# A two-block model on one core: Fourier mixing between two small norms, weight pieces rounded ahead of the first norm, and two 512-column norms taken in two halves

## The chip, the core and the metric

The kernel runs on one core of a Trainium2 chip. TensorE (PE) multiplies, VectorE (DVE) and ScalarE (ACT) do everything between the products, GpSimd (POOL) and SyncE (SP) issue the transfers. The metric is the device time of one execution in microseconds (us); less is better.

## The reference

A first block (two kinds of attention, a cross attention, sixteen experts) makes x; a second block of two layers mixes x (256 tokens, "latent") with a context of 256 tokens. Width 1024, fp32. What the change touches lies in the second block and in the very first norm:

```python
def rmsnorm(x, g):
    y = x * lax.rsqrt(jnp.mean(x * x, axis=-1, keepdims=True) + EPS)
    return y * g

def fourier_mix(u):                       # 256 of the projection's columns
    ug = u.reshape(B, N, F_GROUPS, F_GROUP_DIM)
    return jnp.fft.fft2(ug, axes=(1, 3), norm="ortho").real.reshape(B, N, F_WIDTH)

for l in range(2):
    h  = modulate(rmsnorm(x,  g_norm1[l]), sh1,  sc1)
    hc = modulate(rmsnorm(xc, g_norm1[l]), sh1c, sc1c)
    pf, mq, mk, mv, mo, mg, cq, ckv, kr = split_proj(h @ w_in[l])      # hc likewise
    y_f = fourier_mix(pf)
    ...                                   # mLSTM of q, k, v and the gates mg, both directions
    q  = rmsnorm(cq, g_qn) @ w_uq         # attention through small norms
    kv = rmsnorm(ckv, g_kvn) @ w_ukv
    x  = x + ga1 * (concat([y_f, y_m, y_a]) @ w_out[l])
    x  = x + ga2 * (square(relu(modulate(rmsnorm(x, g_norm2[l]), sh2, sc2) @ w_up[l])) @ w_down[l])
    # layer 0 does the same for the context xc; layer 1 updates the latent half alone
```

## The kernel before

**Layout.** Features lie on the partitions, tokens along the free axis. `res`, `uh` and `ul` hold eight tiles of 128 features by 512 tokens: the slice `CTX` is the context's 256 tokens, `LAT` the latent 256, `ALL` both. Layer 0 works on ALL, layer 1 on LAT but for its keys, values and gates.

**Products in three parts.** Every fp32 weight piece (128 by 1024) is split: ACT copies it, rounded, to `wh` (`hi_part`), DVE subtracts to get the low part `wl` (`lo_part`). Activations are split into `uh` and `ul` in the same way, and `prod` issues three matmuls: high by high, high by low, low by high. The pieces come in one stream through a ring of four slots. A piece n may be rounded when PE has begun piece n-3, and be loaded when the low part of piece n-4 is written. `split(to)`, called by hand in ACT's and DVE's program, sets where in their order each piece is handled (`AHEAD` = 3 pieces before its use).

**Norms.** ACT squares the eight tiles, DVE adds the squares into one slot of `sq`, PE sums over the partitions with a product by ones into bank 7 (`norm` on PE), ACT takes Ln and Exp for `rstd` (`root`). Then DVE scales a tile (`uv`), ACT rounds it to `uh` (`round_u`), DVE makes `ul` (`rest`), and the next matmuls wait for each `ul`. `turn_over` issues matmuls on a constant tile `spin` whose results nobody reads; the table `SPIN` says how many stand before and after the sum of a norm (`"n2_0": (7, 17, 5)`: seven, seventeen, into bank 5).

**Stages that the change touches.** At the start the norm `mix` is followed by `linears("qk", ...)`; ACT's order is `root("mix")`, `split(2)` (three pieces), `round_tiles`. In each layer, after the projections, 32 small products turn the gates' rows (`gcol`), then come the norms `cq` and `ckv`, the products `uq`, `rot`, `kn`, `va`, then the Fourier mixing (`fa`, then `fy`, for each half of the tokens), then the attention's `scores`. At the end of layer 0's mixing stand the eight products `out_0`, whose results DVE adds to `res`, the norm `n2_0` over 512 columns, and `together`, which begins three pieces of the up projection tile by tile as `ul` comes. At the end of layer 0 the last eight down products (`dnb_0`, four turns of a loop in which DVE also reduces the modulation weights, `late_two`, and adds to `res`) are followed by `mod_bias(1)`, the norm `n1_1` over 512 columns, and layer 1's `together`: the gates' piece over ALL, two query pieces over LAT.

**Banks.** Products take banks 0 to 3 in the order of the list `JOBS`; a bank is claimed again once the product four places earlier was emptied.

Of the kernel before, what the change touches and what calls it, by code (L numbers as in the profile page):

```python
# [22 lines left out]
P = 128  # L23
# [71 lines left out]
for _i, (_name, _steps, _halves) in enumerate(NORM_LIST):  # L95
    NORM[_name], STEPS[_name], HALVES[_name] = _i, _steps, _halves
    SQ_AT[_name], ADD_AT[_name] = _sq, _add
    _sq += _steps
    _add += _steps if _name in LOOPED else max(_steps - 2, 0)
# [3 lines left out]
for _l in range(NL):  # L103
    if _l == 0:
        U_STEPS += [("c1_0", 8)]
    U_STEPS += [(f"n1_{_l}", 8), (f"y_{_l}", 10), (f"n2_{_l}", 8)]
# [11 lines left out]
for _name, _n in U_STEPS:  # L118
# [5 lines left out]
        "n2_0": (7, 17, 5), "n1_1": (18, 17, 6), "n2_1": (5, 8, 5),  # L124
        "cq_0": (0, 4, 6), "ckv_0": (4, 6, 6)}
TAIL_SPIN = (6, 8)


OUT_NORMS = [_name for _name, _, _ in NORM_LIST if _name not in V_N and _name not in ("fin1", "ctx")]
# [87 lines left out]
for _l in range(NL):  # L217
    _w = 2 if _l == 0 else 1
    for _phase, _count, _engine in [("mqk", 8, "act"), ("mv", 4, "act"), ("mo", 4, "act"), ("cq", 2, "act"),
                                    ("ckv", 1, "act"), ("pf", 2, "act"), ("uq", 4, "act"), ("rot", 5, "dve"),  # L220
                                    ("kn", 4, "act"), ("va", 4, "act"),
                                    ("fa0", 2, "act"), ("fy0", 2, "act"), ("fa1", 2 * (_w - 1), "act"), ("fy1", 2 * (_w - 1), "act"),
                                    ("mlstm", 4, f"mlstm{_l}"),
                                    ("out", 8, "dve"), ("upa", MC, "act"), ("dna", 8, "dve"), ("upb", MC, "act"), ("dnb", 8, "dve")]:
        JOBS.add(f"{_phase}_{_l}", _count, _engine, _phase != "mlstm")


def build(nc, w_stream, mod_stream, c_rows, ml_dram, gate_dram, table_in, small_in, x_in, mem_in, ctx_in, out):
    with ExitStack() as stack:
# [347 lines left out]
        def _(act):  # L577
# [48 lines left out]

            def round_u(name, i, parts, ready=None):
# [50 lines left out]
            act.wait_ge(S("early_in"), 16)  # L678
            root("mix", P, T, D)
            split(2)  # L680
# [181 lines left out]
            for l in range(NL):  # L862
# [3 lines left out]
                if l:  # L866
                    root(f"n1_{l}", P, 2 * T, D)
                round_mod(l, 0)
# [52 lines left out]
                for d in range(2):  # L921
# [4 lines left out]
                                   ACT.Copy).then_inc(S("gcol_in"), 1)  # L926
                root(f"cq_{l}", P, n, 256)
                square(f"ckv_{l}", 0, ckv[:, :], P, 512)
                root(f"ckv_{l}", P, 512, 128)
# [9 lines left out]
                for s in range(n // T):  # L939
                    sc = slice(cols.start + s * T, cols.start + (s + 1) * T)  # L940
                    for ft in range(2):
                        b = full(act, f"fa{s}_{l}", ft)
                        emptied(act.activation(fa[:, ft, :, :], b[:, :].rearrange("p (a t) -> p a t", a=2),
                                               ACT.Copy), "act")
                    for ft in range(2):
                        b = full(act, f"fy{s}_{l}", ft)
                        emptied(act.activation(yf[:, ft, sc], b[:, 0:T], ACT.Copy), "act")
# [69 lines left out]
                lag = l  # L1017
                for m in range(KT + lag):
                    if m < KT:
                        split(p0 + N_IN2 + min(m, KT - 2) + AHEAD)  # L1020
                    if m >= lag:
                        wait_emptied(act, f"out_{l}", m - lag)
                        square(f"n2_{l}", m - lag, res[:, m - lag, cols], P, n)
                split(p0 + N_IN2 + KT - 1 + AHEAD)
                root(f"n2_{l}", P, n, D)
                round_mod(l, 1)

                for half, name in enumerate("ab"):
# [24 lines left out]
                    else:  # L1053
                        nxt = "n1_1" if l == 0 else "fin2"

                        turns = 4 if l < NL - 1 else 3
# [16 lines left out]
                        if turns == 3:  # L1073
                            hi_at[0] = pd + 12 + AHEAD
                            split(pd + 15)
                            down_squares(3, 3)
                    hi_at[0] = pd + MC + AHEAD
# [4 lines left out]
        def _(pe):  # L1082
# [50 lines left out]
            def norm(name, p, n):  # L1133
# [19 lines left out]
                turn_over(after, spare)  # L1153

# [292 lines left out]
            for l in range(NL):  # L1447
# [3 lines left out]
                if l:  # L1451
                    norm(f"n1_{l}", P, 2 * T)

# [39 lines left out]
                else:  # L1493
                    b = [claim(f"mqk_{l}", j) for j in range(2)]
                    together(f"n1_{l}", p0 - 1, [(bank[4][:, :], P, ALL, True, "ml_g_full"),
                                                 (b[0][0:MD, 0:n], MD, cols, True, "job_full"),
                                                 (b[1][0:MD, 0:n], MD, cols, True, "job_full")])
# [23 lines left out]
                for d in range(2):  # L1521
# [5 lines left out]
                    last.then_inc(S("gcol_full"), 1)  # L1527
                norm(f"cq_{l}", P, n)
                norm_ckv = f"ckv_{l}"

                pe.wait_ge(S("norm_rstd"), NORM[f"cq_{l}"] + 1)
                norm(norm_ckv, P, 512)
# [24 lines left out]

                cn = tab("cn").rearrange("p (b n) -> p b n", b=2)
                sn = tab("sn").rearrange("p (b n) -> p b n", b=2)
                for s in range(n // T):  # L1560
                    c0 = cols.start + s * T
                    for ft in range(2):
                        b = claim(f"fa{s}_{l}", ft)
                        wait_emptied(pe, f"pf_{l}", ft)
                        for nb in range(TB):
                            last = mm(b[:, nb * T:(nb + 1) * T], pf[:, ft, c0 + nb * P:c0 + (nb + 1) * P],
                                      tab("cdsd"), start=True, stop=True)
                        finish(last)
                    for ft in range(2):
                        b = claim(f"fy{s}_{l}", ft)  # L1570
                        wait_emptied(pe, f"fa{s}_{l}", ft)
                        for nb in range(TB):
                            mm(b[:, 0:T], fa[:, ft, nb, 0:P], cn[:, nb, :], start=(nb == 0), stop=False)
                            last = mm(b[:, 0:T], fa[:, ft, nb, P:2 * P], sn[:, nb, :], start=False, stop=(nb == 1))
                        finish(last)
# [83 lines left out]
                for m in range(2, KT):  # L1659
# [5 lines left out]
                norm(f"n2_{l}", P, n)  # L1665
                for half, name in enumerate("ab"):
# [4 lines left out]
                    if half == 0:  # L1671
                        together(f"n2_{l}", pu, [(claim(f"upa_{l}", j)[:, 0:n], P, cols, True, "job_full")
                                                 for j in range(3)])
                        b = claim(f"upa_{l}", 3)
# [21 lines left out]
                    with pe.Fori(0, 4) as i:  # L1696
                        for m in range(2):
# [10 lines left out]
                            last.then_inc(S("job_full"), 1)  # L1708
            norm("fin2", P, T)
# [3 lines left out]
        def _(dve):  # L1713
# [443 lines left out]
    
            for l in range(NL):
# [3 lines left out]
                norm_mod(l, 0)  # L2162
# [198 lines left out]
                for m in range(KT):  # L2361
                    split(p0 + N_IN2 + min(m, KT - 2) + AHEAD)
                    b = full(dve, f"out_{l}", m)
                    emptied(gated(l, m, b, 2), "dve")
                    if m >= 2 + l:
                        add_square(f"n2_{l}", m - 1 - l, P, n)
                for m in range(KT - 1 - l, KT):
                    add_square(f"n2_{l}", m, P, n)
                split(p0 + N_IN2 + KT - 1 + AHEAD)
# [276 lines left out]
```

## Time and profile before

| | us |
|---|---|
| median of 3 runs | 1637.81 (1633.72 to 1641.09) |
| the profiled execution | 1635.65 |
| its span from first to last instruction | 1633.8 |
| PE busy | 1563.7 (96%) |
| DVE busy | 1059.7 (65%) |
| ACT busy | 762.2 (47%) |

PE's busy time counts matmuls of `spin` too, and it is a union of records whose ends are modelled, so 96% doesn't say that 96% of the time does useful work. Starts of neighbouring records tell more than their lengths. An fp32 product (not the split kind) shows as two records. The view of stretches gives the granted TensorE clock as a share: 1.00 is 2.4 GHz, 0.50 is 1.2 GHz.

### The profile page before, as it was taken

What the parts mean: (1) busy time and instruction counts of PE and PEld (TensorE: products, weight loads), DVE (VectorE), ACT (ScalarE), POOL (GpSimd) and SP (SyncE); (2) the same over time, 40 slices, a digit from 0 to 9 for tenths busy, and PEclk for the clock granted to TensorE, in tenths of its full rate; (3) what the DMA queues carried; (4) which work ended last, traced back from release to release, by engine and by line L of the source; (5) the groups of instructions that cost most, each with busy time, mean ns of one, the idle gap of its engine ahead of it and who ended that gap; (6) DMA issues with size and microseconds to landing.
All of it is one profiled execution on the core that took longest, in us unless ns stands there. A gap on an engine that the chain in (4) does not pass through costs nothing.

```text
span 1633.8 us, 27313 instructions
## 1 busy us (share of the span) xinstructions
PE 1563.7 (96%) x9969; PEld 1373.7 (84%) x9969; DVE 1059.7 (65%) x1794; ACT 762.2 (47%) x1309; POOL 99.5 (6%) x165
## 2 busy tenths in 40 slices
PE   7999989999999999999899999999999998999997
PEld 6998788899999997876677888888887885899997
DVE  5567487788888888724765655455557955765564
ACT  5544544444444455344653541244224455665562
POOL 0011000000000000000300100001000001100000
PEclk9999999999999999999999999999999999999999
DMA  7665154487777733330322654455442452146562
GB/s 265 216 225 183 58 178 158 130 289 245 242 245 244 256 105 116 104 90 14 65 104 64 207 191 143 141 193 185 162 154 73 139 130 39 58 159 191 176 191 90
DMA packets 71497, 253.86 MB, mean 155 GB/s; under 512 B 7888, under 2 KB 11120, under 8 KB 71168
## 3 DMA queue, kind: packets, MB, share of 16 engines
q1 hardware_dynamic: 54048, 189.43, 34.9%
q0 software_dynamic: 17376, 63.44, 13.3%
q8 instruction: 49, 0.80, 0.2%
q14 instruction: 24, 0.20, 0.0%
HBM read 251.73 MB, written 1.11 MB: 155 GB/s over the span
## 4 chain that ended last, share of the span: by engine, by line
PE 83%; DVE 10%; ACT 3%; issue 3%; DMA 1%; DVEq 0%; SPq 0%; ACTq 0%
PE pair L1087 82%; ACT wh L586 1%; DVE sq L2299 1%; DVE uv L1761 1%; DVE wl L1720 1%; DVE sq L1801 1%; DVE small L1793 1%; DVE spent L1853 1%; PE pair L1131 1%; DVE uh_f L1853 1%; PE pair L1266 1%; ACT sq L654 0%; DMA uh_f<-in_mods 0%; DMA table<-in_table 0%; DVE ul L1750 0%
## 5 line engine op out<-in xcount | busy, mean ns | idle before, releaser
L1087 PE MATMUL pair<-uh,wh 128*128 128x256 f32 (+3 forms) x1864 | 581.9, 312 | 16.5 <-DVE ul L1750 9.7
L1720 DVE TENSOR_TENSOR wl<-ring,wh 128x1024 fp32r<-128x1024 f32 x350 | 426.6, 1223 | 253.1 <-ACT wh L586 247.1
L1087 PE MATMUL pair<-ul,wh 128*128 128x256 f32 (+3 forms) x1864 | 576.2, 309 | 0.0
L1087 PE MATMUL pair<-uh,wl 128*128 128x256 f32 (+3 forms) x1864 | 576.0, 309 | 0.0
L586 ACT ACTIVATE wh<-ring 128x1024 fp32r<-128x1024 f32 x350 | 366.9, 1052 | 260.4 <-PE pair L1087 253.1
L1087 PEld LDWEIGHTS pair<-uh,wh 128*128 128x128 f32 (+1 forms) x1864 | 346.8, 186 | 45.4 <-issue 17.9
L1087 PEld LDWEIGHTS pair<-uh,wl 128*128 128x128 f32 (+1 forms) x1864 | 347.0, 186 | 23.7
L1087 PEld LDWEIGHTS pair<-ul,wh 128*128 128x128 f32 (+1 forms) x1864 | 346.9, 186 | 22.6
L1087 PE MATMUL pair<-hh,wh 128*128 128x512 f32 (+1 forms) x512 | 172.6, 337 | 0.8
L1087 PE MATMUL pair<-hl,wh 128*128 128x512 f32 (+1 forms) x512 | 172.0, 336 | 0.0
L1087 PE MATMUL pair<-hh,wl 128*128 128x512 f32 (+1 forms) x512 | 172.0, 336 | 0.0
L1087 PEld LDWEIGHTS pair<-hh,wh 128*128 128x128 f32 x512 | 97.1, 190 | 12.0 <-issue 2.0
L1087 PEld LDWEIGHTS pair<-hl,wh 128*128 128x128 f32 x512 | 97.2, 190 | 10.0
L1087 PEld LDWEIGHTS pair<-hh,wl 128*128 128x128 f32 x512 | 97.2, 190 | 9.9
L2420 DVE TENSOR_TENSOR hl<-sq,hh 128x512 f32 (+1 forms) x64 | 35.7, 558 | 92.4 <-ACT hh L1046 92.3
L1041 ACT ACTIVATE sq<-pair 128x512 f32<-128x512 f32 (+1 forms) x64 | 31.3, 489 | 104.4 <-PE pair L1087 104.3
L1087 PE MATMUL pair<-hidh,wl 128*128 128x256 f32 x256 | 72.6, 284 | 0.0
L1087 PE MATMUL pair<-hidh,wh 128*128 128x256 f32 x256 | 72.5, 283 | 0.0
L1087 PE MATMUL pair<-hidl,wh 128*128 128x256 f32 x256 | 72.4, 283 | 0.0
L1087 PE MATMUL pair<-wh,uh 128*128 128x256 f32 (+1 forms) x192 | 57.4, 299 | 3.0 <-ACT qkp L885 3.0
L516 POOL DMA_DIRECT2D uh_f<-in_mods x48 | 36.0, 750 | 397.2 <-DVE macc L1838 218.7
L1838 DVE CUSTOM_DVE_ANT_0 mod_w<-mod_w,mod_c 128x1024 f32<-128x1024 f32 x48 | 58.5, 1218 | 0.0
(279 smaller groups left out, 1991.8 us busy)
## 6 DMA issues: line engine op xcount, KB each, us to landing
ring<-in_w_stream SPq DMA_DIRECT2D x350, 512.0 KB, 3.7
uh_f<-in_mods POOLq DMA_DIRECT2D x48, 512.0 KB, 6.1
mod_w<-in_mods POOLq DMA_DIRECT2D x48, 512.0 KB, 3.8
uv<-c_rows POOLq DMA_DIRECT2D x4, 512.0 KB, 7.1
ml<-ml_dram POOLq DMA_DIRECT2D x4, 512.0 KB, 8.3
table<-in_table SPq DMA_DIRECT2D x1, 1849.5 KB, 12.2
res<-in_x SPq DMA_DIRECT2D x4, 256.0 KB, 4.1
res<-in_mem SPq DMA_DIRECT2D x1, 1024.0 KB, 14.4
```

Source lines behind the costliest of these rows:

```text
L516: pool.dma_start(dst, src).then_inc(S(f"mod_in{g % 2}"), 16)
L586: act.activation(wh[:, s, :], ring[:, s, :], ACT.Copy).then_inc(S("w_hi"), 1)
L1041: act.activation(r, bank[(b0 + j) % 4][:, 0:n], ACT.Relu).then_inc(S("job_emptied_act"), 1)
L1087: ins = pe.matmul(*operands, **flags)
L1131: pe.matmul(bank[b], spin[:, 0:P], spin[:, :], start=True, stop=True)
L1266: last = pe.transpose(bank[6][:, to * P:(to + 1) * P], prob[i % 2][:, j * P:(j + 1) * P], ident)
L1720: tt(wl[:, s, :], ring[:, s, :], wh[:, s, :].bitcast(F32), ALU.subtract).then_inc(S("w_lo"), 1)
L1761: last = stt(o, src, g, r, ALU.mult, ALU.mult)
L1793: dve.tensor_reduce(smv(i, 0, 0, g), b, AX_X, ALU.max, negate=True).then_inc(S("sm_max"), 1)
L1838: return dve.tensor_tensor_reduce(out=mod_w[l][k], in0=mod_w[l][k], in1=mod_c[l][which], scale=1.0, scalar=0.0, op0=ALU.mult, op1=ALU.add, ...
L1853: last = dve.tensor_tensor_reduce(out=w if which == 0 else spent_to, in0=w, in1=c[which], scale=1.0, scalar=0.0, op0=ALU.mult, op1=ALU.add ...
L2420: tt(hl[:, d, 0:n].rearrange("p a b -> p (a b)"), sq[:, 2 + j % 2, 0:n], hh[:, d, 0:n].rearrange("p a b -> p (a b)").bitcast(F32), ALU.sub ...
```

## The change

Four edits, and what follows from them:

- **Start.** ACT's `split(2)` stands ahead of `root("mix")`.
- **Small norms.** `JOBS` gets `fa` and `fy` ahead of `uq`, and all three engines follow. Layer 0: after the sum of `cq`, PE does `fa`, `fy` of the context; after the sum of `ckv`, `fa`, `fy` of the latent half. Layer 1: `fa` after the sum of `cq`, `fy` after the sum of `ckv`. ACT empties them between its roots. The spins of both norms in layer 0 go.
- **`n2_0` in halves.** `out_0` 6 and 7 are computed over CTX first, then over LAT into banks 4 and 5. The context's sum, root, tiles and rounding come ahead of the latent's; DVE and ACT have the last adds, squares and one `split` between them. The first three pieces of the up projection run over CTX (two of them tile by tile, then the third), then over LAT. 24 spins go.
- **`n1_1` in halves.** The loop over down products has three turns; the last turn is written out. Its second product runs over CTX, then LAT into bank 6. DVE does the last `late_two` and `mod_bias(1)` ahead of the last adds. Layer 1's gates run over CTX tile by tile, with the latent's sum after the fourth tile, then 8 spins, then gates over LAT with the two query pieces. 35 spins go, 8 come.

```diff
+            split(2)
             root("mix", P, T, D)
-            split(2)
             round_tiles("mix", LAT)
...
+            def half_sum(name, c, squares):
+                pe.wait_ge(S("norm_add"), ADD_AT[name] + (5 if name == "n2_0" else 6))
+                pe.wait_ge(S("norm_sq"), SQ_AT[name] + squares)
+                for k, slot in enumerate((3, 0, 1)):
+                    last = mm(bank[7][:, c], ones, sq[:, slot, c], start=(c is CTX and k == 0), stop=(k == 2),
+                              skip_group_check=True)
+                last.then_inc(S("half_ms" if c is CTX else "norm_ms"), 1)
...
                 norm(f"cq_{l}", P, n)
+                spectrum(0, "fa")
+                if l == 0:
+                    spectrum(0, "fy")
                 pe.wait_ge(S("norm_rstd"), NORM[f"cq_{l}"] + 1)
-                norm(norm_ckv, P, 512)
+                norm(f"ckv_{l}", P, 512)
+                if l == 0:
+                    spectrum(1, "fa")
+                    spectrum(1, "fy")
+                else:
+                    spectrum(0, "fy")
...
+                    b = {m: claim("out_0", m) for m in (6, 7)}
+                    for c in (CTX, LAT):
+                        for m in (6, 7):
...
+                            last.then_inc(S("out_ctx" if c is CTX else "job_full"), 1)
+                            if c is LAT and m == 6:
+                                half_sum("n2_0", CTX, 8)
...
+                        for k in range(KT):
+                            for j in range(2):
+                                up(j, k, CTX)
+                            if k == 2:
+                                half_sum("n2_0", LAT, 10)
+                        pe.wait_ge(S("w_lo"), pu + 3)
+                        for k in range(KT):
+                            up(2, k, CTX)
+                        for k in range(KT):
+                            for j in range(3):
...
+                                last = up(j, k, LAT)
...
+                    for k in range(KT):
+                        pe.wait_ge(S("u_l"), U_AT["n1_1c"] + k + 1)
+                        prod(bank[4][:, CTX], p0 - 1, k, uh[:, k, CTX], ul[:, k, CTX], k == 0, k == KT - 1,
+                             skip_group_check=True)
+                        if k == 3:
+                            half_sum("n1_1", LAT, 9)
+                    turn_over(8, 5)
...
+            def half_tiles(l, k2, add_last, then):          # DVE
+                half_tile(l, k2, CTX, 0)
+                half_tile(l, k2, CTX, 1)
+                half_rest(l, k2, CTX, 0)
+                half_tile(l, k2, CTX, 2)
+                half_rest(l, k2, CTX, 1)
+                add_last()
+                half_tile(l, k2, CTX, 3)
+                half_rest(l, k2, CTX, 2)
+                then()
+                for k in range(4, KT):
+                    half_tile(l, k2, CTX, k)
+                    half_rest(l, k2, CTX, k - 1)
+                for k in range(KT):
+                    half_tile(l, k2, LAT, k)
...
+                            root_half("n1_1", CTX)          # ACT
+                            round_half(1, 0, CTX, 0)
+                            round_half(1, 0, CTX, 1)
+                            split(pd + 18)
+                            act.wait_ge(S("job_emptied_dve"), b1 + 7)
+                            act.activation(sq[:, 1, LAT], res[:, 7, LAT], ACT.Square).then_inc(S("norm_sq"), 1)
+                            for k in range(2, 4):
+                                round_half(1, 0, CTX, k)
+                            root_half("n1_1", LAT)
+                            for k in range(4, KT):
+                                round_half(1, 0, CTX, k)
+                            for k in range(KT):
+                                round_half(1, 0, LAT, k)
```

`n2_0` has the same order on ACT, with `split(po + KT + 2)` in the place of `split(pd + 18)`, where `po` is the first of the `out_0` pieces.

## Rows read from the trace of the kernel before

**Rows 1.** The page: the chain that ended last, shares of the span by engine.
```profile
PE 83%; DVE 10%; ACT 3%; issue 3%; DMA 1%; DVEq 0%; SPq 0%; ACTq 0%
```
**Rows 2.** Stretches, PE alone: from:to, length, busy (records), granted clock, DMA share, GB/s.
```profile
842.30:876.60 34.30, 34.30 (x152) 1.00 0.48 169
1418.30:1435.90 17.60, 17.60 (x152) 1.00 0.67 209
19.30:22.70 3.40, 3.32 (x15) 0.51 1.03 403
1336.90:1343.70 6.80, 5.42 (x11) 0.50 0.84 69
1246.50:1258.70 12.20, 12.17 (x73) 1.00 0.06 9
```
**Rows 3.** Timeline, the first 20 us: start, length, engine, line, tiles, count [idle before <-releaser].
```profile
11.66 5.12 PE L1131 MATMUL pair<-spin 128*128 128x512 f32 x19
...
13.15 2.94 ACT L586 ACTIVATE wh<-ring 128x1024 fp32r<-128x1024 f32 x3
14.22 3.50 DVE L1720 TENSOR_TENSOR wl<-ring,wh 128x1024 fp32r<-128x1024 f32 x3 [6.78 <-ACT wh L586]
...
17.63 1.27 DVE L1761 SCALAR_TENSOR_TENSOR uv<-res,table,rstd 128x256 f32<-128x256 f32 x3
...
19.38 0.55 PE L1087 MATMUL pair<-uh,wh 128*128 128x256 f32 x1 [2.60 <-DVE ul L1750]
```
**Rows 4.** The first four ring transfers (issued at 3.3 to 4.7 us): issue to landing.
```profile
DMA to landing us min/median/max: 6.4/7.6/8.8
```
**Rows 5.** Timeline of PE, layer 0 from the sum of cq to the scores.
```profile
720.96 1.98 PE L1087 MATMUL pair<-sq,table 128*128 128x512 f32 x4
...
727.64 7.03 PE L1087 MATMUL pair<-cq,lw 128*96 128x512 f32 x16
...
744.58 1.89 PE L1087 MATMUL pair<-table,pf 128*128 128x256 f32 x8
746.38 3.69 PE L1087 MATMUL pair<-table,sq 128*128 128x256 f32 x16
...
755.24 1.89 PE L1087 MATMUL pair<-ka,qa 96*128 96x256 f32 x8
```
**Rows 6.** Timeline of ACT beside it: the square of ckv, the last va emptied.
```profile
724.24 0.62 ACT L612 ACTIVATE sq<-ckv 128x512 f32<-128x512 f32 x1
...
744.78 0.49 ACT L938 ACTIVATE va<-pair 128x384 f32<-128x384 f32 x1 [0.15 <-PE pair L1087]
```
**Rows 7.** Timeline of PE, layer 1, the same stretch, from the gates' small products.
```profile
1332.28 3.31 PE L1087 MATMUL pair<-table,rows_buf 4*128 4x4 f32 x32
1335.52 1.13 PE L1087 MATMUL pair<-sq,table 128*128 128x256 f32 x4
1338.28 2.05 PE L1087 MATMUL pair<-sq,table 128*128 128x512 f32 x2 [1.62 <-ACT sq L612]
1340.12 5.41 PE L1087 MATMUL pair<-cq,lw 128*96 128x256 f32 x16
...
1360.76 1.88 PE L1087 MATMUL pair<-ka,qa 96*128 96x512 f32 x4
```
**Rows 8.** Timeline of PE, DVE and ACT around the norm n2_0.
```profile
876.51 1.79 PE L1131 MATMUL pair<-spin 128*128 128x512 f32 x7
...
881.65 2.46 DVE L1761 SCALAR_TENSOR_TENSOR uv<-res,gmod,rstd 128x256 f32<-128x256 f32 x6 [1.19 <-ACT rstd L625]
882.57 2.51 ACT L635 ACTIVATE uh<-uv,modv 128x256 fp32r<-128x256 f32 x6 [0.95 <-DVE uv L1761]
...
885.05 0.47 PE L1087 MATMUL pair<-uh,wh 128*128 128x512 f32 x1 [0.93 <-DVE ul L1752]
```
**Rows 9.** Timeline of PE around the norm n1_1.
```profile
1235.09 4.24 PE L1131 MATMUL pair<-spin 128*128 128x512 f32 x18
...
1246.53 0.47 PE L1087 MATMUL pair<-uh,wh 128*128 128x512 f32 x1 [1.02 <-DVE ul L1752]
```

More of the change, by code:

```diff
@@ L1015, in _ @@
                 head_round(MH - 1)
[L1017 to L1026, printed above, removed]
+                po = p0 + N_IN2
@@ L1658, in _ @@
                     finish(output(early[m], m, KT - 1))
-                for m in range(2, KT):
+                for m in range(2, KT - (2 if l == 0 else 0)):
                     b = claim(f"out_{l}", m)
@@ L1695, in _ @@
                     pe.wait_ge(S("hid_lo"), ready + MC // 2)
-                    with pe.Fori(0, 4) as i:
+                    halved = l == 0 and half
+                    with pe.Fori(0, 3 if halved else 4) as i:
                         for m in range(2):
@@ L1708, in _ @@
                             last.then_inc(S("job_full"), 1)
+                    if halved:
+                        for m in range(2):
+                            pe.wait_ge(S("job_emptied_dve"), 6 + (e_dve - 2 + m))
+                            for c in (CTX, LAT) if m else (ALL,):
+                                b = bank[6 if c is LAT else (b0 + m) % 4]
+                                for part in range(2):
+                                    n_piece = pd + 12 + 2 * m + part
+                                    if c is CTX and part:
+                                        pe.wait_ge(S("w_lo"), n_piece + 1)
+                                    elif not (c is LAT and part == 0):
+                                        parts(n_piece)
+                                    for k in range(8):
+                                        last = prod(b[:, c], n_piece, k, hh[:, part * 8 + k, c], hl[:, part * 8 + k, c],
+                                                    part + k == 0, part == 1 and k == 7)
+                                    if c is LAT and part == 0:
+                                        half_sum("n1_1", CTX, 8)
+                                last.then_inc(S("down_ctx" if c is CTX else "job_full"), 1)
             norm("fin2", P, T)
@@ L2462, in down_turn @@
                                 tt(sq[:, 3, 0:n], sq[:, 3, 0:n], sq[:, j, 0:n], ALU.add).then_inc(S("norm_add"), 1)
-                    turns = 3 if ends else 4
+                    turns = 3 if nxt else 4
                     with dve.Fori(0, turns) as i:
```

289 lines of the change are left out of this document (226 added, 63 removed).

## The prediction

> **What bounds the kernel now.** I read the chain that ended last first: 83% of it is PE [rows 1]. So a stage is shortened only by what lies on PE's path, and I then read, stage by stage, what PE waits for. The waits are short. What the change can win is mostly hidden as busy time: matmuls on `spin` that fill the time of a norm. Around `n2_0` the last output product ends at 876.51, where spins begin, and the next real matmul starts at 885.05: 8.5 us [rows 8]. Around `n1_1` it is 1235.09 to 1246.53, 11.4 us [rows 9]. Then I read pitches, since record lengths overlap: 150 split matmuls (and two at the edges) take 34.3 us at 512 columns, 0.229 each, and 17.65 us at 256 columns, 0.118 each [rows 2]. A plain fp32 product of 512 columns takes 0.86 (eight `uq` products, 16 records, in 6.9), one of 256 columns 0.43 (four of `fa` in 1.75) [rows 5]. DVE and ACT need 0.40 for an operation on 256 columns (six in 2.46 and in 2.51) [rows 8], 1.14 and 0.95 for the low and the high part of a weight piece [rows 3]. From the end of a PE record to its reader's start I take 0.2.
>
> **Start.** The norm's sum ends at 12.3; today `root` runs, then three high parts at 13.15, then three low parts to 17.7, then the tiles, and PE starts at 19.38, having idled 2.60 [rows 3]. Landings: issued from 3.3 to 4.7, landing after 6.4 to 8.8 [rows 4], so the first piece is there at 9.7, the fourth at 13.5, the third, between them, near 12.2. With `split(2)` ahead the high parts end at 10.7, 12.0, 13.2, the root at 14.1, the low parts at 14.5, the first `ul` at 16.1. Now the 19 spins are late next: the last ends at 16.8 less its tail, 16.6 [rows 3]. PE starts at 16.6, a gain of 2.75. The clock was at 0.51 from 19.3 to 22.7, behind the 2.60 of idling [rows 2]; without the idling it should not fall: 15 matmuls at 0.213 become 0.118, 1.45 more. Sum **4.2**; 2.0 if the clock falls nevertheless and the third piece lands 0.75 later, since ACT then stands on it with `root` behind it and DVE behind that. SP's later loads queue behind transfers that fill the DMA until 25 us either way.
>
> **Small norms, layer 0.** From the sum of `cq` at 720.96 to the scores at 755.24 [rows 5]. The Fourier products (744.58 to 755.24, 10.65) move ahead of `uq`. PE: sum to 722.7; `fa` to 724.4; ACT is at its root and the square of `ckv` until 724.86 [rows 6], and two copies of 0.5 follow, so `fy` runs 725.4 to 728.9 after a wait of 1.0; sum of `ckv` to 729.7; latent `fa` to 731.45; ACT's root ends at 731.3, its copy at 731.9, a wait of 0.5; `fy` to 735.4. `uq` thus starts 7.75 later than 727.64, and `va` ends at 752.35. There the Fourier work used to cover ACT's emptying of the last `va` (744.78 plus 0.49, 0.7 behind PE [rows 6]); now the scores wait for it: 753.05. Gain **2.2**; between 0.8 (each new wait doubled) and 2.6.
>
> **Small norms, layer 1.** 1335.52 to 1360.76 [rows 7]. At full clock: sum to 1336.4, `fa` to 1338.1 in what is 1.62 of idling, sum of `ckv` to 1339.05, `fy` to 1342.5, `uq` (eight products of 0.43) to 1345.95, the 10.05 from there to the old place of `fa` (1360.76 less 5.33, half of layer 0's Fourier time) to 1356.0, 0.7 for `va`: 1356.7, a gain of 4.05. But from 1336.9 to 1343.7 the clock was at 0.50 [rows 2], behind 3.3 us of four-column products and the idling. The small products stay, only the idling goes. I take one fall of 3.4, as long as the one at the start, which costs half: **2.35**. Ends: 0.6 (6.8 us at half) and 4.05.
>
> **`n2_0`.** Before: 865.5 (876.51 less 48 x 0.229) to 901.5 (885.05 plus 72 x 0.229), 36.0 [rows 8]. After: 240 half matmuls x 0.118 are 28.3, two half sums of three products x 0.43 are 2.6, in all 30.9, and waits. No product is shown before in this order, so I lay DVE, ACT and PE side by side with the 0.40s. The context's sum (874.0 to 875.3) runs ahead of the last latent product, its root ends at 876.5, the first `ul` is ready as that product ends, at 878.15. Third tile: DVE adds the last latent output (behind four operations), ACT squares it before it rounds the tile: PE waits 1.15. Fifth tile: the latent's sum stands on PE after the third, its root stands on ACT ahead of the fifth tile's rounding: 1.45. The other tiles come every 0.80 against 0.71 of matmuls: 0.45 in all. So 33.9, gain **2.15**. Ends 3.0 and 0. The up projection's following piece needs its low part at 904, and DVE, free at 895, has it.
>
> **`n1_1`.** Before: the last down product starts at 1224.1 (1235.09 less 48 x 0.229 [rows 9]); the three-piece group ends at 1258.7 [rows 2], 34.6. After: 96 half matmuls 11.3, sums 2.6, context gates 24 x 0.118 = 2.8, eight spins 1.8, latent 72 x 0.118 = 8.5: 27.0. The modulation reductions (5 us of DVE) now run under the seventh product, which hides them. Waits: context tiles come from DVE every 0.80 and keep PE for 0.35 only, 0.45 each, four times; third tile 1.5 (last add and square, as above); fourth 1.6 (DVE's low part of a weight piece, 1.14, stands before it); fifth 2.2 (the latent's sum waits for the fourth on PE, its root blocks ACT). 7.1 in all, 34.1: a gain of 0.5. And in these 11 us PE works 4.1, sparser than what preceded either fall in [rows 2], where spins filled the time before. I take one fall, on the latent's sum or on the spins and latent products behind it: 1.6. Net **-1.1**; ends +1 and -3.5.
>
> The halves themselves cost 192 pairs x (2 x 0.118 - 0.229) = 1.3 us, which is inside the sums above. The Trainium skill (TensorE: Matmul & The Clock Gate, section "Wait — 56ns, not 53.3ns?") gives matmuls a fixed 2.5 ns beside their columns; by it the 192 would cost 0.5 us and the forecast would be 0.8 lower; these rows show 7 ns for each extra matmul, not 2.5, and no lower price is taken.
>
> **Sum.** 4.2 + 2.2 + 2.35 + 2.15 - 1.1 = 9.8. The profiled execution of 1635.65 would become 1625.9; the median stands 2.2 above it, and the forecast goes from the median: 1637.8 - 9.8 = **1628.0**. All low ends together give a gain near 0, all high ends 14.9. About 0.5% (8.2 us) is what a measurement of this kernel can tell from no change.
>
> **Rivals.**
> - *The clock holds in every filled stage.* For it: from 842 to 877 and beyond, dense work holds 1.00 [rows 2]. Against: layer 1's small products and the sparse gates remain. 4.2 + 2.2 + 4.05 + 2.15 + 0.5 = 13.1: 1624.7. Chance 0.14.
> - *The halves pay nothing*, so that half of the change doesn't do what it says: the order on ACT and DVE (last add, last square, a weight piece and the latent's root among the context's tiles) makes PE wait as long as it spun. For it: the waits that I count are already 3 and 7 us. `n2_0` 0, `n1_1` -3.5, the others as forecast: 5.2, 1632.6. Chance 0.28.
> - *Slower: half clock in the place of the spins.* The spins kept the clock at 1.00 through both large norms. If it falls behind all five places for 6.8 us, as once before [rows 2], that costs 5 x 3.4 = 17 against the 13.1: 1641.7. It turns into a loss from 26 us at half clock, into a measurable one from 43. Against: three of the five stages become denser. Chance 0.06, half of it beyond 0.5%.
>
> **How the numbers follow.** The forecast has 0.52; its own spread, from the unknown waits, is about 3 us to either side, so that two thirds of it lie more than 8.2 us below the median. Faster: 0.35 + 0.14 + 0.05 = 0.54; slower 0.03; within 0.5% 0.43. The range 1623 to 1635 takes in the first two rivals and leaves out the third and the extreme ends.
>
> **What would show it.** In the changed kernel PE's first split matmul at 16.6 and no stretch at half clock before 30 us; the scores of layer 0 some 32 us behind the sum of `cq` (34.3 before), those of layer 1 22 to 23 behind (25.2); the three up pieces ending 33.9 behind the start of output 6, with waits of 1.1 and 1.5 at the third and fifth context tile; layer 1's first group ending 34 to 36 behind the start of the last down product. Wrong it would be if the start gains under 2 (pieces landing late), if context tiles come slower than one in 0.80, or if half clock shows in `n2_0`.

## The result, and the profile after

The changed kernel takes 1628.36 us (median of 9 runs, 1625.50 to 1636.96), the kernel before, on the same chip, 1637.76 (9 runs, 1633.72 to 1641.09): ratio 0.995, 95% interval 0.993 to 0.997. The forecast was 1628.0. The profiled execution's span went from 1633.8 to 1626.5. That the total fits hides two terms that missed in opposite directions, so the parts have to be looked at one by one.

The page: PE's row (busy, share, count), and the chain's shares, to set beside [rows 1].

```profile
PE 1556.9 (96%) x10114; PEld 1377.4 (85%) x10114; DVE 1059.2 (65%) x1791; ACT 764.7 (47%) x1316; POOL 99.5 (6%) x165
...
PE 83%; DVE 10%; ACT 3%; issue 3%; DMA 1%; DVEq 0%; SPq 0%; ACTq 0%
```

PE bounds it as before. **Start**, timelines of ACT and of PE (start, length, engine, line, tiles, count [idle before <-releaser]), beside [rows 3]:

```profile
9.80 1.06 ACT L591 ACTIVATE wh<-ring 128x1024 fp32r<-128x1024 f32 x1 [1.95 <-DMA ring<-in_w_stream]
11.02 1.06 ACT L591 ACTIVATE wh<-ring 128x1024 fp32r<-128x1024 f32 x1 [0.16 <-DMA ring<-in_w_stream]
12.31 1.06 ACT L591 ACTIVATE wh<-ring 128x1024 fp32r<-128x1024 f32 x1 [0.23 <-DMA ring<-in_w_stream]
...
11.25 5.96 PE L1218 MATMUL pair<-spin 128*128 128x512 f32 x19
17.05 0.28 PE L1174 MATMUL pair<-uh,wh 128*128 128x256 f32 x1
```

ACT now waits for each piece (the ring's DMA is the releaser three times), and PE starts when the last spin ends, with no idle time in front of it; the 193rd split matmul starts at 41.57 instead of 45.49, 3.9 us earlier. **Small norms**, PE in layer 0, beside [rows 5], then the sum of `cq` and the first scores of layer 1, beside [rows 7]:

```profile
713.84 3.31 PE L1174 MATMUL pair<-table,rows_buf 4*128 4x4 f32 x32
717.08 3.67 PE L1174 MATMUL pair<-sq,table 128*128 128x512 f32 x4
720.59 1.89 PE L1174 MATMUL pair<-table,pf 128*128 128x256 f32 x8
723.29 3.69 PE L1174 MATMUL pair<-table,sq 128*128 128x256 f32 x16 [0.81 <-ACT sq L956]
...
751.11 1.10 PE L1174 MATMUL pair<-ka,qa 96*128 96x256 f32 x4 [0.63 <-issue]
...
1329.33 1.13 PE L1174 MATMUL pair<-sq,table 128*128 128x256 f32 x4
...
1350.78 1.10 PE L1174 MATMUL pair<-ka,qa 96*128 96x512 f32 x2 [0.63 <-issue]
```

From the sum of `cq` to the scores it is 34.03 us (34.28 before). The sum of four records took 3.67 where it took 1.98 in [rows 5]. Layer 1 went from 25.24, with 6.8 us at half clock [rows 2, rows 7], to 21.45 at full clock (1329.33 to 1350.78), so its 3.8 us are not the order's alone (see the repeats below).

Stretches of the changed kernel (from:to, length, PE busy, PEld, DVE, ACT, POOL, granted clock, DMA share, GB/s): layer 0's sum, what stands ahead of it, `n2_0`, `n1_1` and a part of it.

```profile
717.10:720.50 3.40, 3.40 (x5) 1.49 (x5) 0.00 (x0) 0.26 (x2) 1.49 (x2) 0.50 0.28 72
712.30:717.10 4.80, 4.80 (x41) 4.22 (x39) 0.00 (x0) 0.85 (x3) 0.00 (x0) 1.00 0.32 109
...
859.70:893.60 33.90, 31.89 (x254) 31.00 (x253) 20.55 (x45) 14.94 (x29) 0.00 (x0) 1.00 0.20 61
...
1216.20:1252.40 36.20, 31.71 (x213) 29.22 (x212) 21.28 (x47) 13.99 (x27) 0.53 (x1) 0.86 0.23 74
1232.50:1242.70 10.20, 7.44 (x23) 6.03 (x24) 5.58 (x15) 4.06 (x9) 0.00 (x0) 0.50 0.17 51
```

`n2_0` takes 33.8 us (36.1 before), at full clock. PE waits at its third and fifth context tile:

```profile
874.83 0.38 PE L1174 MATMUL pair<-uh,wh 128*128 128x256 f32 x1 [0.79 <-DVE ul L1933]
...
879.03 0.38 PE L1174 MATMUL pair<-uh,wh 128*128 128x256 f32 x1 [1.22 <-DVE ul L1933]
```

`n1_1` takes 36.3 (34.5 before), 10.2 of them at half clock. Its waits on PE, and what ACT and DVE do in them:

```profile
1231.40 0.39 PE L1174 MATMUL pair<-uh,wh 128*128 128x256 f32 x1 [1.14 <-DVE ul L1933]
...
1233.33 0.58 PE L1174 MATMUL pair<-uh,wh 128*128 128x256 f32 x1 [1.30 <-DVE ul L1933]
...
1234.13 2.76 PE L1174 MATMUL pair<-sq,table 128*128 128x256 f32 x6
1238.83 0.58 PE L1174 MATMUL pair<-uh,wh 128*128 128x256 f32 x1 [1.93 <-DVE ul L1933]
...
1230.01 0.42 ACT L1156 ACTIVATE sq<-res 128x256 f32<-128x256 f32 x1 [0.39 <-DVE res L2586]
1230.34 0.89 ACT L659 ACTIVATE uh<-uv,modv 128x256 fp32r<-128x256 f32 x2
1236.93 0.47 ACT L640 ACTIVATE rstd<-pair,table 128x256 f32<-128x256 f32 x1 [5.71 <-PE pair L1174]
...
1231.26 1.22 DVE L1901 TENSOR_TENSOR wl<-ring,wh 128x1024 fp32r<-128x1024 f32 x1
```

The latent's last square is done at 1230.43, but its sum stands on PE behind the fourth context tile, whose `ul` waits for the low part at 1231.26. So the sum starts 3.7 us late, at half clock, and ACT, standing at the root for 5.71, rounds no fifth tile.

The gains by stage are 3.9, 0.25, 3.8, 2.3 and -1.8, together 8.5. Elsewhere, in code that the change does not touch, the changed kernel's profile lacks a fall at 804 us (3.4 us at half clock before), and layer 1's two up halves take 45.2 us each instead of 44.2 and 43.5, a loss of 2.7. With some 1.6 for the first, that makes 7.4, against 7.3 of span. Falls of the clock ahead of layer 0 (at 306 us before; at 222, 304 and 591 us here) cancel out: the sum of `cq` in layer 0 is as much earlier as the 193rd split matmul.

### The profile page after: what moved, and what is told of

Its sections match the earlier page's. It is cut to its first block, busy times and chain, and to the rows that moved or that the text cites. A ratio compares the mean times of both kernels' runs of the same rounds, so it can differ in the third digit from the quotient of the medians.

```text
span 1626.5 us, 27578 instructions
## 1 busy us (share of the span) xinstructions
PE 1556.9 (96%) x10114; PEld 1377.4 (85%) x10114; DVE 1059.2 (65%) x1791; ACT 764.7 (47%) x1316; POOL 99.5 (6%) x165
## 4 chain that ended last, share of the span: by engine, by line
PE 83%; DVE 10%; ACT 3%; issue 3%; DMA 1%; DVEq 0%; SPq 0%; ACTq 0%
PE pair L1174 81%; ACT wh L591 1%; DVE sq L2521 1%; PE pair L1218 1%; DVE wl L1901 1%; DVE sq L1982 1%; DVE small L1974 1%; DVE spent L2034 1%; DVE uh_f L2034 1%; DVE uv L1942 1%; PE pair L1362 1%; ACT sq L678 0%; DMA uh_f<-in_mods 0%; DVE ul L1931 0%; DVE ul L1933 0%
## 5 line engine op out<-in xcount | busy, mean ns | idle before, releaser
L1174 PE MATMUL pair<-uh,wh 128*128 128x256 f32 (+3 forms) x1912 | 591.7, 309 | 16.5 <-DVE ul L1933 8.6
L1174 PE MATMUL pair<-uh,wl 128*128 128x256 f32 (+3 forms) x1912 | 585.1, 306 | 0.0
L1174 PE MATMUL pair<-ul,wh 128*128 128x256 f32 (+3 forms) x1912 | 584.1, 305 | 0.0
L1174 PEld LDWEIGHTS pair<-uh,wh 128*128 128x128 f32 (+1 forms) x1912 | 355.5, 186 | 43.5 <-issue 10.7
L1174 PEld LDWEIGHTS pair<-uh,wl 128*128 128x128 f32 (+1 forms) x1912 | 355.9, 186 | 21.7
L1174 PEld LDWEIGHTS pair<-ul,wh 128*128 128x128 f32 (+1 forms) x1912 | 355.6, 186 | 21.1
L1174 PE MATMUL pair<-hh,wh 128*128 128x256 f32 (+1 forms) x528 | 175.7, 333 | 0.8
L1174 PE MATMUL pair<-hh,wl 128*128 128x256 f32 (+1 forms) x528 | 174.8, 331 | 0.0
L1174 PE MATMUL pair<-hl,wh 128*128 128x256 f32 (+1 forms) x528 | 174.8, 331 | 0.0
```

The source lines that it names most:

```text
L1174: ins = pe.matmul(*operands, **flags)
```

## The experiments

Each is an edit of the changed kernel; medians are of the runs named. The executions of one kernel scatter by 3 to 12 us, so a stage's term is read from the profile's stage first. The halves of `n2_0` were not undone by themselves; their gain rests on the stage in the profiles of before and after.

**Undo `n1_1`.** The fourth edit back to the code before.

```diff
-        "n2_1": (5, 8, 5)}
+        "n1_1": (18, 17, 6), "n2_1": (5, 8, 5)}
...
-HALVED = ("n2_0", "n1_1")
+HALVED = ("n2_0",)
...
+                if l:
+                    norm(f"n1_{l}", P, 2 * T)
...
+                    together(f"n1_{l}", p0 - 1, [(bank[4][:, :], P, ALL, True, "ml_g_full"),
...
```

> The changed kernel with its fourth edit alone taken back: n1_1 over 512 columns again, its 35 spins, the four-turn loop, the modulation reductions and the three-piece group of layer 1 as before. Theory (the halves of n1_1 cost time by their own waits and by half clock): from the start of the last down product to the end of the group 34.6 us instead of 36.1, granted clock 1.00 there, total 1.5 below the changed kernel, near 1626.9. Rival (the edit also disturbs what follows, so that the 2.7 us lost in layer 1's up projection, code unchanged, come from it): the two up halves of layer 1 go back to 44.2 and 43.5 us for 384 matmuls (45.2 each in the changed kernel) and the total is 4 below, near 1624.2. Rival (the stage is no worse in halves): total equal to the changed kernel's or above it.

The stage: 34.5 us at full clock.

```profile
1218.10:1252.60 34.50, 32.29 (x160) 25.91 (x159) 24.65 (x53) 13.14 (x24) 0.53 (x1) 1.00 0.21 65
```

The stage answers as expected, 1.8 us shorter. The up halves of layer 1 stay at 45.5 and 45.2, so the 2.7 us do not come from this edit. The total, 1629.74 (5 runs, 1625.49 to 1632.33), does not show the 1.8: the profile has 6.8 us at half clock near 160 us and 3.4 beside layer 1's sum of `cq` that the changed kernel's has not, so totals of so few runs can't tell it.

**Early sums.** One number in two places.

```diff
-                        if k == 3:
+                        if k == 1:
                             half_sum("n1_1", LAT, 9)
...
-                            if k == 2:
+                            if k == 1:
                                 half_sum("n2_0", LAT, 10)
```

> The changed kernel with only the latent's sums moved on PE: n1_1's from behind the fourth context tile to behind the second, n2_0's from behind the third to behind the second. Theory (the place of the sum makes the fifth-tile wait: in the changed kernel the latent's square ends at 1230.43, its sum starts only at 1234.13, and its root stands on ACT ahead of the fifth tile's rounding): the fifth-tile wait of n1_1 falls from 1.93 to under 0.5, the stage from 36.1 to between 31.5 and 33; n2_0's fifth-tile wait falls from 1.22 to under 0.3, its stage from 33.7 to 32.5 to 33; total 4 to 6 below the changed kernel, near 1623. Rival (tiles come from DVE no faster, DVE's low part of a weight piece among them): the wait moves to the third and fourth tile, n1_1's stage stays above 35, total within 1.5 of the changed kernel.

PE in `n1_1` of this kernel, then its stretch:

```profile
1232.93 1.53 PE L1174 MATMUL pair<-sq,table 128*128 128x256 f32 x6 [0.32 <-ACT sq L1156]
...
1235.69 0.39 PE L1174 MATMUL pair<-uh,wh 128*128 128x256 f32 x1 [0.87 <-DVE ul L1933]
...
1236.48 0.39 PE L1174 MATMUL pair<-uh,wh 128*128 128x256 f32 x1 [0.16 <-DVE ul L1933]
...
1218.50:1249.40 30.90, 28.91 (x214) 26.87 (x213) 21.25 (x47) 14.16 (x27) 0.53 (x1) 1.00 0.25 83
```

`n1_1` takes 30.8, 5.4 less than with the late sum and 3.7 less than with no halves; the fifth tile's wait is 0.16, and the clock stays full. It lies below the 31.5 to 33 that was expected. `n2_0` takes 32.3 (33.8). The median is 1620.63 (5 runs, 1619.04 to 1631.37), 7.7 below the changed kernel's, where 4 to 6 was expected. The rival, that DVE's pace would keep the wait, is left with the 0.87 at the fourth tile.

**Spins in the waits of `n1_1`.**

```diff
                             half_sum("n1_1", LAT, 9)
+                        turn_over((0, 4, 5, 6, 0, 1, 1, 0)[k], 5)
                     turn_over(8, 5)
```

> The changed kernel with spins put into PE's waits between n1_1's context tiles: 4, 5, 6 behind the second, third and fourth tile, one each behind the sixth and seventh; nothing else changed. Theory (PE's sparse work there brings the half clock, which lengthens the latent's sum to 2.76 us and all behind it): granted clock 1.00 from 1220 to 1255, the sum of the latent in 1.4 us, the stage 1.5 to 2.5 us shorter than 36.1, total 1.5 to 2.5 below the changed kernel. Rival (the order on DVE and ACT alone sets the time): the clock may hold, but the stage stays within 0.6 of 36.1, or grows if a spin is late.

```profile
1233.62 1.46 PE L1174 MATMUL pair<-sq,table 128*128 128x256 f32 x6
1234.73 1.74 PE L1218 MATMUL pair<-spin 128*128 128x512 f32 x6
1237.02 0.39 PE L1174 MATMUL pair<-uh,wh 128*128 128x256 f32 x1 [0.55 <-DVE ul L1934]
...
1216.00:1249.90 33.90, 32.69 (x230) 29.43 (x229) 21.30 (x47) 14.01 (x27) 0.53 (x1) 1.00 0.24 76
```

The clock holds, the sum takes 1.46 instead of 2.76, the stage 33.9 instead of 36.3: half clock cost 2.4 us here, and the order of sum and root some 3 more (33.9 to 30.8). The cost does not follow the length of the fall: three other profiles with the late sum (the changed kernel's second, the repeat with the start undone, and the one with the Fourier move undone, all below) have 6.8 us at half clock in this stage instead of 10.2, and it takes 36.3, 36.7 and 36.1 us all the same. The median, 1627.00 (8 runs, 1624.71 to 1634.73), is 1.4 below the changed kernel's, about what was expected.

**Undo the start.**

```diff
+            root("mix", P, T, D)
             split(2)
-            root("mix", P, T, D)
```

> The changed kernel with the first edit taken back: split(2) stands behind root again. Theory: the first split matmul goes from 17.05 back to 19.4, the half clock at 19 to 23 comes back, the end of the 192 qk matmuls goes from 40.2 to 44.1, and the total is 3.9 above the changed kernel, near 1632.3. Rival (the gain at the start is taken back later, where PE waits for a transfer or another engine anyway): the start is later by 3.9, the total by less than 2.

PE's first split matmul, and the granted clock behind it:

```profile
19.04 0.55 PE L1174 MATMUL pair<-uh,wh 128*128 128x256 f32 x1 [2.83 <-DVE ul L1931]
...
18.60:22.00 3.40, 2.96 (x14) 2.99 (x15) 3.40 (x10) 2.08 (x6) 0.00 (x0) 0.50 1.05 401
```

Idling and half clock are back, the 193rd split matmul starts at 44.94 (41.57 in the changed kernel), and the median is 1634.17 (10 runs, 1631.14 to 1638.60): the start's gain reaches the end of the kernel. That the total moves by 5.8 and not by 3.4 or 3.9 lies within the scatter. Where the 193rd split matmul starts also varies between executions: 39.5 to 42.8 us in the eight profiles with this edit and 19 spins, 44.8 to 45.5 in the three without it. The means, 41.1 and 45.1, lie 3.9 apart.

**Undo the Fourier move.** `JOBS`, `SPIN` and the order on ACT and PE as before.

```diff
                 norm(f"cq_{l}", P, n)
-                spectrum(0, "fa")
-                if l == 0:
-                    spectrum(0, "fy")
...
+                for s in range(n // T):
+                    spectrum(s, "fa")
+                    spectrum(s, "fy")
```

> The changed kernel with its second edit taken back: fa and fy stand behind va again, the ten spins of cq_0 and ckv_0 are back. Theory (the Fourier products fill PE's waits in the small norms, and a granted clock that falls behind the four-column products takes part of it back in some executions): layer 0's stretch from the sum of cq to the scores 34.3 us where the clock stays full, 36 with one fall of 3.4 (the changed kernel 34.0, with one fall); layer 1's 23.2 where it stays full, 25.2 with a fall of 6.8 (the changed kernel 21.45, without); the total 3.5 to 4.5 above the changed kernel, near 1632.4. Rival (the order of the small norms buys nothing, its gain in the one profile of before was the clock's alone): layer 0 and layer 1 within 0.6 of the changed kernel's at the same clock, the total within 1.5.

Layer 0 and layer 1, sum to scores:

```profile
717.60:754.00 36.40, 35.76 (x111) 20.41 (x112) 9.10 (x22) 13.66 (x26) 2.19 (x3) 0.92 0.20 44
...
1333.40:1359.00 25.60, 23.34 (x74) 13.51 (x74) 8.57 (x22) 10.41 (x22) 2.89 (x4) 0.84 0.35 40
```

36.4 and 25.6, with 6.8 and 10.2 us at half clock; the median is 1635.52 (10 runs, 1631.37 to 1639.30). Against the changed kernel's first profile the two stretches make 6.5 us; the medians lie 7.2 apart, where 3.5 to 4.5 was expected. The expected 34.3 held for full clock only, and the fall came, of 6.8 us and not of 3.4; in layer 1 it was 10.2 and not 6.8.

**Three repeats, unaltered**, to see what one profile leaves to chance.

> The changed kernel once more, unaltered, for a second profile. Theory (the pitch of 113 or 118 ns in layer 1's up halves and part of the falls of the clock are settled anew in each execution, not by the code): the two up halves differ from the first profile's 45.2 and 45.2 in at least one, the fall behind the four-column products is there in layer 0 in one length or another, and n1_1's stage repeats at 36.1 to 36.4 with 0.86 of the clock. Rival (the code sets the pitch): 45.2 and 45.2 again.

> The changed kernel a third time, unaltered. If the execution settles the pitch, 43.5 or 45.2 for the second up half of layer 1; if the kernel settles it, 45.2 a third time. n1_1's stage 36.1 to 36.4 as in both profiles; layer 0's small norms 32.3 without a fall of the clock, 33.8 to 34.2 with one.

> undo_start once more, unaltered. Its PE program is the changed kernel's; in its first profile the second up half of layer 1 took 43.5 us for 384 matmuls, in both profiles of the changed kernel 45.2. If the execution settles the pitch anew, either value may come, and over this and the next two runs at least one kernel shows both; if the kernel as a whole (its addresses on other engines, its timing) settles it, 43.5 again. The start shows the idling and the half clock again: first split matmul near 19.0, idle 2.6 to 2.9.

Times 1629.19, 1630.80 and 1636.08. `n1_1` repeats: 36.26, 36.28 and 36.65. The small norms do not. Us at half clock beside the sum of `cq`, and the stretch from that sum to the scores:

| profile | layer 0: half clock, stretch | layer 1: half clock, stretch |
|---|---|---|
| before | none, 34.28 | 6.8, 25.24 |
| undo Fourier | 6.8, 36.39 | 10.2, 25.61 |
| changed | 3.4, 34.03 | none, 21.45 |
| changed, second | none, 32.33 | 6.8, 23.81 |
| changed, third | 6.8, 34.14 | none, 21.45 |

The sum of `cq` and the first scores of layer 0 in the second profile, without a fall, beside [rows 5]:

```profile
715.49 1.98 PE L1174 MATMUL pair<-sq,table 128*128 128x512 f32 x4
...
747.82 1.53 PE L1174 MATMUL pair<-ka,qa 96*128 96x256 f32 x6 [0.63 <-issue]
```

At an equal clock the move is worth 1.95 (34.28 to 32.33) and 2.25 (36.39 to 34.14) in layer 0. In layer 1 it is 1.4 at 6.8 us of half clock (25.24 to 23.81); the old order was not seen at full clock there. So of the 3.8 us that layer 1 gained in the first profile some 2.4 are a fall that did not come in that execution.

The pitch of layer 1's second up half is 45.2 us in two profiles of the changed kernel and 43.5 in the third. The rival, that the code alone sets it, falls. That each execution settles it anew is not shown: the third profile comes from another chip than the second, and no kernel is known to have shown both values on one chip. The chip alone does not set it either: both chips show both values, with different kernels.

**Four-column products apart.** The 32 products of the gates' rows stand in a row ahead of the sum of `cq`; here those of the second direction go behind `fa`, on PE and on ACT.

```diff
-                for d in range(2):
+                def turned(d):
                     pe.wait_ge(S("ml_rows"), 2 * l + d + 1)
...
+                turned(0)
                 norm(f"cq_{l}", P, n)
                 spectrum(0, "fa")
+                turned(1)
```

> The changed kernel with only the four-column products parted, as in best2: those of the second direction behind the fa products. Theory (32 four-column products in a row bring the half clock in most executions, and best2's steadiness against best1 comes from parting them): no stretch at half clock within 5 us of them in either layer; layer 0's wait at fy (0.81) filled; median 2 to 5 below the changed kernel, near 1625; n1_1 unchanged at 36.1 to 36.3 with its 10 us at half. Rival (best2's full clock there was chance): a fall of 3.4 or more at the sum of cq in layer 0, as in seven of the eight other profiles, and a median within 1.5 of the changed kernel's.

Layer 0 and layer 1 around them:

```profile
711.00:748.00 37.00, 35.44 (x136) 21.29 (x136) 9.11 (x22) 14.44 (x30) 2.19 (x3) 1.00 0.18 41
1310.00:1348.00 38.00, 36.73 (x191) 27.00 (x190) 14.69 (x27) 20.57 (x40) 2.32 (x4) 1.00 0.40 104
```

Full clock in both layers. The median, 1626.25 (6 runs, 1622.68 to 1632.31), is 2.1 below the changed kernel's, which the scatter of either does not bear out: the ratios to the kernel before, 0.9935 (0.9914 to 0.9956) and 0.995 (0.993 to 0.997), overlap. The stages tell more. From the first four-column product to the scores, layer 0 takes 35.24 us here, 35.57 in the changed kernel without a fall (second profile) and 37.27 with one (first). Layer 1 takes 25.26 here, 24.69 without a fall (first) and 27.85 with one (second). So at full clock parting gains 0.3 in one layer and loses 0.6 in the other; what it pays beyond that, it pays by the clock. In the twelve profiles with the products in a row, a fall begins beside the sum in nine in layer 0 and in eight in layer 1; in the two with them apart (this one and the last kernel below) in none of four places. Where the other five executions of this kernel ran at half clock is not recorded.

**The moves together.** The first kernel takes the early sums, fills and thins the spins, and takes two waits away in the small norms; the second parts the four-column products as well.

```diff
-SPIN = {"mix": (0, 19, 6), "sb": (0, 6, 6), "xattn": (6, 8, 6), "ffn": (6, 8, 6),
+SPIN = {"mix": (0, 15, 6), "sb": (0, 6, 6), "xattn": (6, 8, 6), "ffn": (6, 8, 6),
...
+                        turn_over((0, 0, 3, 1, 1, 1, 1, 0)[k], 5)
-                    turn_over(8, 5)
+                    turn_over(2, 5)
...
-                wait_emptied(pe, f"va_{l}", 3)
+                    if i == units.start + 2:
+                        wait_emptied(pe, f"va_{l}", 3)
```

> The changed kernel with five small moves: the latent's sums behind the second context tile (as in early_sum); in n1_1 three spins behind the third tile, one behind each of the next four, and 2 instead of 8 ahead of the latent tiles; 15 instead of 19 spins at the start; in layer 0 ACT copies fa ahead of the square of ckv; PE waits for the emptied va not ahead of the scores but ahead of the first product that reads va. Theory, by stages at full clock: n1_1 29.4 us (early_sum 30.84), n2_0 32.3, the first split matmul as soon as the first low part is there (0.7 earlier than with 19 spins), layer 0's wait at fy from 0.81 to under 0.2, the wait ahead of the scores from 0.63 to nothing in both layers; total 3.5 below early_sum, near 1617. Rival (fewer spins let the clock fall in n1_1 or behind the start, 3.4 to 10 us at half): n1_1 above 31 with granted clock under 0.95, total no lower than early_sum's 1620.6.

> best1 once more, unaltered. Pitch: 43.5 for the second up half again if the kernel settles it. The four-column products stand in a row here: a fall of the clock at the sum of cq in layer 0 is expected (6.8 us in the first profile), and one in layer 1 about as often as not; n1_1's stage 29.5 again at full clock.

> best1 with the 32 four-column products of each layer parted: those of one direction stay ahead of the sum of cq, those of the other go behind the fa products, where PE waits for ACT's copies. Theory (the clock falls behind the four-column products because 3.3 us of them stand in a row: 717.1 in the changed kernel, at 718 to 722 in four more profiles, at 1326 to 1337 in three of six): no stretch at half clock within 5 us of them in either layer, and 0.8 us of waiting in layer 0 filled; total 2 to 4 below best1, near 1614. Rival (what they are followed by doesn't matter, the falls come from elsewhere): a fall of 3.4 to 6.8 near the sum of cq in layer 0 as before, total within 1.5 of best1.

The first: 1618.93 (4 runs, 1616.80 to 1622.28), `n1_1` in 29.5 us, and 1617.75 for its repeat. In layer 0 it shows 6.8 us at half clock in the first profile and none in the repeat, in layer 1 3.4 in both. The second: 1616.82 (4 runs, 1615.71 to 1618.60), ratio 0.9869 (0.9848 to 0.9890) to the kernel before. PE in its layer 0, and the stretches of both layers and of `n1_1`:

```profile
712.32 1.94 PE L1181 MATMUL pair<-table,rows_buf 4*128 4x4 f32 x16
714.19 1.98 PE L1181 MATMUL pair<-sq,table 128*128 128x512 f32 x4
716.01 1.89 PE L1181 MATMUL pair<-table,pf 128*128 128x256 f32 x8
717.84 1.94 PE L1181 MATMUL pair<-table,rows_buf 4*128 4x4 f32 x16
719.71 3.72 PE L1181 MATMUL pair<-table,sq 128*128 128x256 f32 x16
...
712.30:747.00 34.70, 33.77 (x131) 20.46 (x131) 9.10 (x22) 13.99 (x30) 1.49 (x2) 1.00 0.14 36
1311.00:1338.00 27.00, 26.36 (x128) 18.18 (x127) 10.37 (x24) 11.86 (x27) 1.48 (x2) 1.00 0.38 74
...
1210.20:1239.70 29.50, 28.91 (x215) 26.50 (x214) 21.23 (x47) 14.17 (x27) 0.53 (x1) 1.00 0.24 73
```

The wait of 0.81 at `fy` is gone. In the first kernel ACT's new order had left 0.29 of it, in the second, and in the changed kernel with the products apart, the second direction's products fill it. The median of the second kernel lies 2.1 below the first's, where 2 to 4 was expected; with four runs each, which overlap, this is not told from chance. From the first four-column product to the scores, layer 0 takes 34.44 us in the second kernel; in the first it takes 37.14 with a fall and 34.27 without (the repeat).

## Why the prediction was right or wrong

- **The total**: 1628.36 against 1628.0 is closer than the parts deserve. The stages of the profile gain 8.5 and its span 7.3, where 9.8 was forecast; 9.4 is the distance of two medians whose runs spread by 7 and 11 us. In the profile layer 0 gained 1.95 less than forecast and layer 1 1.45 more, each for the most part by a fall of the clock that came or did not come in that execution: that they cancel is luck.
- **What bounds it** was right: PE's share of the chain is 83% in both, and the gains and losses of the stages on PE add up to the span's.
- **Start**: right in mechanism and size. First matmul 17.05 (16.6 forecast), 3.9 us gained of 4.2. The spins are late next, as said: the first `ul` is there at 16.14, PE starts 0.9 later. The miss lay in the 19 spins' length: 5.96 us here, 5.12 in [rows 3]. It varies: 4.69 to 6.04 in the eight profiles with this edit and 19 spins, where PE starts 0.15 to 1.6 behind the first `ul`. With 15 spins it starts 0.14 to 0.19 behind it, in three profiles.
- **Small norms, layer 0**: the sum of steps was right (34.28 less 2.2 is 32.1, the second profile shows 32.33; waits 0.81, 0.29 and 0.63 against 1.0, 0.5 and 0.7). What failed is that no fall of the clock was counted there, because the one profile of before had none. Two of three profiles of the changed kernel have one, and one of two of the old order.
- **Small norms, layer 1**: at full clock it took 21.45; the forecast was 25.24 less 4.05, 21.2. The fall of 3.4 that the forecast took is in no profile of the changed kernel (none, 6.8, none); over the eight profiles in which layer 1's small norms are the changed kernel's it is 3.0 in the mean. The reason given for the old fall, "3.3 us of four-column products and the idling", was half misread: the clock fell at 1336.9 [rows 2], and the 1.62 of idling ends at 1338.28 [rows 7], so it began at 1336.66, 0.2 us ahead of the fall. What stood before it are the four-column products, and those remained.
- **`n2_0`**: right, 33.8 against 33.9, with waits of 0.79 and 1.22 at the third and fifth tile against 1.15 and 1.45. Its matmuls show a second pitch that the prediction did not know (below): 33.3 in the second profile.
- **`n1_1`**: the waits were a little over-sized (1.14, 1.30 and 1.93 against 1.5, 1.6 and 2.2), the fall was under-sized: 10.2 us at half clock instead of 3.4, worth 2.4 instead of 1.6. Without it 34.1 was forecast, and 33.9 measured with the spins. The prediction named the latent's sum as what stands in the way on PE and ACT; that this alone, moved by two tiles, would turn the loss of 1.8 into a gain of 3.7 it did not work out.
- **The rival of the halves that pay nothing** is half true: one pays 2.3, the other costs 1.8. **The rival of half clock in the spins' place** came true in two of its five places in the first profile: in `n1_1`, for longer than it assumed (10.2), and in layer 0, for shorter (3.4).
- **The price of halves**: a 256-column matmul at 0.118 against 0.229 for 512 columns was right for most stretches. The Trainium skill (TensorE: Matmul & The Clock Gate, section "Wait — 56ns, not 53.3ns?") gives 2.5 ns beyond the columns. The rows here show 7 to 11 (pitches of 113 and 118 ns, where 256 columns at 2.4 GHz are 106.7), and the forecast was right not to take it.

## What to carry to other kernels

When work is cut in halves to hide a norm, look for the one operation that the second half's chain begins with, and issue it as soon as its inputs are there: here the second sum, two tiles earlier on PE, was worth 5.4 us (2.4 of them the clock's), while the cut without it cost 1.8. Where the granted clock falls in some executions and not in others, a stage's time is read together with its granted clock, in several executions, since one profile shows either outcome. Matmuls of a few columns in a row are cheap to interleave with dense ones: at full clock the stretches changed by 0.3 us less and 0.6 us more.

## What the runs showed of the hardware that was not expected

**The clock fell behind busy work.** In the 4.8 us ahead of the fall at 717.1 PE's records leave no idle time at all (4.80 of 4.80, with modelled ends), but 3.3 of it are products of four columns. The Trainium skill (TensorE: Matmul & The Clock Gate, section "HAM oscillation — how this bites in real kernels") lays such falls to idle gaps of PE; this fall stands behind none. Parting the products went with full clock in four of four places, in two executions; why a row of them brings the fall is not shown.

**Two pitches of the same matmuls.** Split matmuls of 256 columns in the same loop start every 113 ns or every 118 ns for a whole stretch at full clock. Second up half of layer 1, 384 matmuls: the kernel before, the changed kernel, and the changed kernel's third profile (383 of them).

```profile
1533.50:1577.00 43.50, 43.50 (x384) 43.50 (x385) 25.47 (x32) 31.98 (x61) 0.00 (x0) 1.00 0.59 184
...
1524.50:1569.70 45.20, 45.20 (x384) 45.20 (x385) 25.59 (x32) 31.98 (x61) 0.00 (x0) 1.00 0.57 177
...
1528.50:1572.00 43.50, 43.44 (x383) 43.44 (x384) 25.38 (x32) 31.98 (x61) 0.00 (x0) 1.00 0.60 182
```

DVE's and ACT's work beside it is the same (25.4 to 25.6 and 31.98 us). In the first up half of the changed kernel 94 starts come at 113 ns, then one 0.48 us and one 0.22 us behind the last, and the rest at 118. At 113 ns two halves cost no more than one product of 512 columns (0.227 to 0.229 us), at 118 ns more. What chooses between the two is open.
